# Short state-space calculations in the first modulation, and the turns of the state tiles cut in four and set between the steps of layer 1's linear attention

## What is computed

```python
lam = lax.complex(a_re, a_im)
dt = jnp.exp(log_step)[:, None]
a_bar = jnp.exp(lam * dt)
b_bar = ((a_bar - 1.0) / lam)[..., None] * lax.complex(b_re, b_im)
...
_, states = lax.associative_scan(s5_combine, (a_elems, bu), axis=1)
```

## Time and profile before

| | us |
|---|---|
| median of 3 runs | 1559.35 |
| lowest, highest | 1557.97, 1561.33 |
| the profiled execution | 1564.3 |
| its span (first to last instruction) | 1562.5 |
| PE busy in the span | 1386.5 |
| PEld busy | 1160.0 |
| DVE busy | 853.4 |
| POOL busy | 733.4 |
| ACT busy | 637.7 |

### The profile page before, as it was taken

One profiled execution on the slowest core, in us unless ns is written; L12 is line 12 of the kernel. 1 busy time (PEld: TensorE's weight loads), 2 busy tenths in 40 slices (PEclk: granted clock), 3 DMA queues, 4 the chain that ended last, 5 costly groups with the idle time before them and its releaser, 6 DMA issues.

```text
span 1562.5 us, 24541 instructions
## 1 busy us (share of the span) xinstructions
PE 1386.5 (89%) x10288; PEld 1160.0 (74%) x10288; DVE 853.4 (55%) x1213; ACT 637.7 (41%) x1002; POOL 733.4 (47%) x512
## 2 busy tenths in 40 slices
PE   5798999999999999688779899978799888799997
PEld 1654688777676887464768789968688777799996
DVE  1567415332333430756677666569899635488811
ACT  2445322433332333445325554656422123555542
POOL 0520044332222643140595767747645204499984
PEclk9899999999999999899899999989899999999998
DMA  8320133343443432130334334525222133355552
GB/s 335 120 68 14 42 95 94 108 175 122 161 161 120 137 95 81 40 95 28 108 94 135 108 122 132 162 84 178 79 83 82 56 95 109 94 185 181 188 176 82
DMA packets 49119, 180.79 MB, mean 116 GB/s; under 512 B 5489, under 2 KB 6513, under 8 KB 48625
## 3 DMA queue, kind: packets, MB, share of 16 engines
q1 hardware_dynamic: 48864, 177.13, 34.9%
q10 hardware_dynamic: 144, 2.10, 0.3%
HBM read 178.16 MB, written 1.05 MB: 115 GB/s over the span
## 4 chain that ended last, share of the span: by engine, by line
PE 67%; DVE 18%; ACT 5%; DMA 4%; POOL 3%; issue 2%; SPq 0%; ACTq 0%; DVEq 0%
PE ps L368 17%; PE ps L370 16%; PE ps L369 16%; PE ps L372 15%; DMA panels<-weights 3%; POOL panels_r L412 2%; DVE work L1830 2%; POOL panels_r L413 2%; ACT panels_hi L402 1%; PE ps L889 1%; DMA const_sb<-constants 1%; DVE small L937 1%; DVE work L732 1%; DVE work L1260 1%; DVE work L761 0%
## 5 line engine op out<-in xcount | busy, mean ns | idle before, releaser
L412 POOL TENSOR_TENSOR panels_r<-panels,panels_hi 128x512 fp32r<-128x512 f32 x254 | 376.0, 1480 | 808.5 <-ACT panels_hi L402 806.7
L369 PE MATMUL ps<-h_sb_r,panels_hi 128*128 128x256 f32 (+1 forms) x1408 | 453.3, 322 | 0.0
L402 ACT ACTIVATE panels_hi<-panels 128x1024 fp32r<-128x1024 f32 x254 | 267.5, 1058 | 416.8 <-PE ps L370 233.4
L413 POOL TENSOR_TENSOR panels_r<-panels,panels_hi 128x512 fp32r<-128x512 f32 x254 | 370.6, 1459 | 0.0
L368 PE MATMUL ps<-hi_sb_r,panels_hi 128*128 128x512 f32 (+1 forms) x784 | 279.8, 357 | 40.7 <-POOL panels_r L413 24.1
L369 PEld LDWEIGHTS ps<-h_sb_r,panels_hi 128*128 128x128 f32 x1408 | 276.9, 197 | 17.8 <-issue 0.7
L370 PE MATMUL ps<-hi_sb_r,panels_r 128*128 128x512 f32 (+1 forms) x784 | 273.2, 348 | 0.0
L368 PEld LDWEIGHTS ps<-hi_sb_r,panels_hi 128*128 128x128 f32 x784 | 153.9, 196 | 66.7 <-issue 19.2
L368 PE MATMUL ps<-h_sb_r,panels_hi 128*128 128x256 f32 x624 | 183.6, 294 | 12.1 <-DVE h_sb_r L594 7.6
L368 PE MATMUL ps<-work_r,panels_hi 128*128 128x256 f32 (+1 forms) x560 | 182.9, 327 | 10.2 <-POOL panels_r L413 6.0
L370 PE MATMUL ps<-h_sb_r,panels_r 128*128 128x256 f32 x624 | 179.5, 288 | 0.0
(11 more groups left out here) (323 smaller groups left out, 1820.4 us busy)
## 6 DMA issues: line engine op xcount, KB each, us to landing
panels<-weights SPq DMA_DIRECT2D x328, 512.0 KB, 3.6
x_sb<-x_in SPq DMA_DIRECT2D x1, 2048.0 KB, 8.1
x_sb<-x_in ACTq DMA_DIRECT2D x1, 2048.0 KB, 8.7
const_sb<-constants SPq DMA_DIRECT2D x1, 1216.0 KB, 10.6
out<-x_sb SPq DMA_DIRECT2D x2, 512.0 KB, 3.1
vec_sb<-vectors SPq DMA_DIRECT2D x1, 725.0 KB, 11.9
small<-c_in SPq DMA_DIRECT2D x1, 8.0 KB, 1.6
```

The costliest lines, as they stand in the source:

```text
L369: pe.matmul(o, lhsT.hi, rhs.lo, start=False, stop=False)
L402: act.activation(panels_hi[:, m:m + PANEL * P], panels[:, n:n + PANEL * P], ACT.Copy).then_inc(panel_rounded, 1)
L412: pool.tensor_tensor(panels_r[:, at:at + half], panels[:, at:at + half], panels_hi[:, m:m + half], ALU.subtract)
L413: pool.tensor_tensor(panels_r[:, at + half:at + 2 * half], panels[:, at + half:at + 2 * half], panels_hi[:, m + half:m + 2 * half], ALU.su ...
```

## The change

The short calculations (`s5_steps`, `s5_angles`, `s5_polar`, `s5_factors`) go from the head of layer 1 to the first modulation: the exponential ahead of the first `mod_copy` and the angles ahead of the first `mod_use`; the polar part behind that `mod_copy` and the factors behind that `mod_use`. They keep their results in other columns of `small`. The seven turns of 128x4096 become 28 units of 128x1024, seven per quarter of the state tiles, each waiting for the one before (u = 7q + n, with n as before). They leave the head; eight groups of them stand between VectorE's steps in the merge of layer 1. `whole_turns`, the buffer between, has the size of a quarter and lies in the context's half of `x_sb`. Each of the first four `s5_tables` waits for its own quarter.

```diff
@@ (these functions move here, ahead of first_modulation)
+        kept, brief = Room(small, 420), Room(small, 320)
+        mag, f_hi, f_lo, c_re, c_im = [kept(S5T) for _ in range(5)]
+        dt, th, turn, s_r, c_r = [brief(S5T) for _ in range(5)]
...
+        half_col = region(small, 36, 1)
+
+        def s5_steps(act):
+            act.wait_ge(vectors_loaded, 16)
+            act.activation(dt, vec("log_step"), ACT.Exp).then_inc(steps_done, 1)
+
+        def s5_angles(dve):
+            step = steps["dve"]
+            dve.memset(half_col, half_pi)
+            dve.wait_ge(vectors_loaded, 16)
+            dve.wait_ge(steps_done, 1)
...
@@ first_modulation
             def scalar(act):
+                s5_steps(act)
                 for i in range(len(MOD_FIRST)):
                     mod_copy(act, i, 6)
+                    if i == 0:
+                        s5_polar(act)
 
             def vector(dve):
+                s5_angles(dve)
                 for i, n in enumerate(MOD_FIRST):
                     mod_use(dve, i, 0, n, 7)
+                    if i == 0:
+                        s5_factors(dve)
@@ trunk
-            by_act, by_dve, head_products, head_scalar, head_vector = projection(f"inputs{l}", tiles, first=clear_pads, then=windows,
-                                        aside={("scalar", 0): s5_steps, ("vector", 0): s5_angles, ("scalar", 1): s5_polar,
-                                               ("vector", 1): s5_factors, ("vector", 3): s5_turns(0, 3), ("vector", 9): s5_turns(3, 4),
-                                               ("vector", 10): s5_turns(4, 5), ("vector", 11): s5_turns(5, 6)} if last else {})
+            by_act, by_dve, head_products, head_scalar, head_vector = projection(f"inputs{l}", tiles, first=clear_pads, then=windows)
@@ gla_and_merge
             def vector(dve):
                 steps["dve"](dve.memset(attn, 0.0))
                 inputs.head.vector(dve)
                 decay_minima(dve)
-                if inputs.turns is not None:
-                    inputs.turns(6, 7)(dve)
                 split_y(dve, 0)
...
                 mixes(dve, MIXES[l][0], MIXES[l][1])
+                turn(dve, 0, 6)
                 decayed(dve, 0)
                 mixes(dve, MIXES[l][1], cut[0])
                 scores_taken(dve, 0)
+                turn(dve, 6, 8)
                 mixes(dve, cut[0], cut[1])
                 states_summed(dve, 0)
+                turn(dve, 8, 11)
                 mixes(dve, cut[1], cut[2])
...
                 scores_taken(dve, 1)
+                turn(dve, 11, 13)
                 mixes(dve, cut[3], cut[4])
                 states_summed(dve, 1)
+                turn(dve, 13, 17)
                 mixes(dve, cut[4], cut[5])
                 outputs_added(dve)
+                turn(dve, 17, 20)
                 mixes(dve, cut[5], cut[6])
                 norm_inverse(dve)
+                turn(dve, 20, 22)
                 mixes(dve, cut[6], cut[7])
...
                 mixes(dve, MIXES[l][3], 3 * KD)
+                turn(dve, 22, 28)
@@ s5_turns, s5_tables
-        turns, whole_turns = cos_t, region(work, 10240, S5T, T)
+        turns, whole_turns = cos_t, of_context[:, 2:6, :]
...
-                t = each(const("step"), S5T)
-                for n in range(first, end):
-                    if n:
-                        dve.wait_ge(turned5, n)
+                t = each(const("step"), 4)
+                for u in range(first, end):
+                    n, q = u % 7, u // 7
+                    g = slice(4 * q, 4 * q + 4)
+                    part, of_step = turns[:, g, :], (f_hi, f_lo)[n // 3 % 2][:, g]
+                    if u:
+                        dve.wait_ge(turned5, u)
...
-                    if i == 0:
-                        act.wait_ge(turned5, 7)
+                    act.wait_ge(turned5, 7 * (i + 1))
```

More of the change, by code:

```diff
@@ new lines, in build @@
+        half_pi = 3.1415925 / 2
+        full = 6.283185
+        steps_done, arg_ready = sem("s5_steps_done"), sem("arg_ready")
+        half_col = region(small, 36, 1)
[7 more added lines that the diff above has]
+            dve.wait_ge(steps_done, 1)
+            step(dve.tensor_tensor(mag, vec("a_re"), dt, ALU.mult))
+            step(dve.tensor_tensor(th, vec("a_im"), dt, ALU.mult))
+            step(dve.tensor_scalar(turn, th, 1.0 / two_pi, None, ALU.mult))
+            step(dve.tensor_scalar(turn, turn, whole, None, ALU.add))
+            step(dve.tensor_scalar(turn, turn, -whole, None, ALU.add))
+            for c in (pi_a, pi_b, pi_c):
+                step(dve.scalar_tensor_tensor(th, turn, -c, th, ALU.mult, ALU.add))
+            step(dve.tensor_scalar(th, th, -3.1415925, 3.1415925, ALU.max, ALU.min))
+            step(dve.tensor_scalar(turn, th, 1.0 / two_pi, None, ALU.mult))
+            step(dve.tensor_scalar(f_hi, turn, 1.5 * 2 ** 11, None, ALU.add))
+            step(dve.tensor_scalar(f_hi, f_hi, -1.5 * 2 ** 11, None, ALU.add))
+            dve.tensor_tensor(f_lo, turn, f_hi, ALU.subtract).then_inc(arg_ready, 1)
@@ L1516, in scalar, with turn @@
                 gates(act, GATES[l][2], 3 * KD)
+            def turn(dve, first, end):
+                if inputs.turns is not None:
+                    inputs.turns(first, end)(dve)
             def vector(dve):
@@ L1570, in build @@
         sin_t, cos_t = s5_room(S5T, T), s5_room(S5T, T)
-        turns, whole_turns = cos_t, region(work, 10240, S5T, T)
         of_context = x_sb[:, :].rearrange("p (k s t) -> p k s t", s=2, t=T)[:, :, 1, :]
-        one = Room(small, 420)
-        dt, mag, th, turn, f_hi, f_lo, c_re, c_im, s_r, c_r = [one(S5T) for _ in range(10)]
-        two_pi = 2.0 * float(np.pi)
-        pi_a = 6.28125
-        pi_b = float(np.float32(round((two_pi - pi_a) * 2 ** 20) / 2 ** 20))
-        pi_c = float(np.float32(two_pi - pi_a - pi_b))
@@ L1649, in vector @@
                     elif n in (1, 5):
[L1650 removed]
+                        ins = dve.tensor_scalar(whole_turns, part, whole, None, ALU.add)
                     else:
[L1652 removed]
+                        ins = dve.scalar_tensor_tensor(part, whole_turns, whole, part, ALU.subtract, ALU.subtract)
                     ins.then_inc(turned5, 1)
```

86 lines of the change are left out of this document (33 added, 53 removed).

## The result

The changed kernel takes **1549.16 us** (median of 9 runs, 1542.57 to 1554.63) against 1560.75 (9 runs, 1556.36 to 1561.88) for the kernel before on the same chip: ratio 0.9932, 95% interval 0.9911 to 0.9953. Gains in us are worked out from this ratio here, of 1560 us: 10.6 less. Run once more, later and beside other kernels, it gave 1550.36 us (6 runs) and 0.9934 (0.9911 to 0.9958), 10.3 us less. The forecast was 11.4 us less.

What follows compares the result with a forecast made beforehand. The prediction blamed TensorE's gaps in layer 1's head on late POOL, delayed by ScalarE's wait and whole turns. Head gain 22.1 less merge cost 10.7 gave 11.4 us: 1559.35 - 11.4 = 1548.0 us, its own range 1542 to 1555.

Steps and rivals of the forecast that it cites:

- The head gives 22.1: Layer 1's head: three TensorE gaps of 8.59, 1.90 and 7.71 us and the half-clock restarts go, 22.1 us less.
- the stand: Layer 1's head: ScalarE waits 9.91 us for small angle operations; removing this ends TensorE's first gap, 8.59 us plus 2.5 clock.
- Units 0 to 5, 6.0: Merge, ahead of the first decayed: taking turns with POOL delays VectorE, so TensorE waits some 6.0 us for the scores.
- Clock behind it, 1.4: Merge: TensorE restarts at a lower clock after its wait for the first scores, costing 1.4 us.
- Units 11 and 12, 2.3: Merge, ahead of mix 11 and the summed states: with two POOL pieces they exceed their 1.99 us cover, costing 2.3 us.
- Units 20 and 21, 1.0: Merge, ahead of a mix and the norm's product: half of a 2.2 us excess over cover counted, 1.0 us.
- Merge, 10.7: Layer 1's merge: the moved units cost 6.0 + 1.4 + 2.3 + 1.0 = 10.7 us.
- Last group, 0: Units 22 to 27, behind the merge's last mix: VectorE is idle 28.12 us there, so they cost 0.
- POOL becomes the merge's bound: Rival, merge: units before the last group hold POOL off, adding 22.8 us; 1571 us, slower, chance 0.06.
- The gaps hold: Rival, merge: POOL's backlog misses units 0 to 5, later groups are covered, merge costs 2.9; 1540 us, chance 0.22.
- the second and third gap stay: Rival, layer 1's head: something other than turns keeps POOL late, only 8.59 + 2.5 comes back; 1559 us, chance 0.05.
- POOL is met everywhere: Rival, merge: 75% of units 6 to 21 each meet a POOL piece, merge costs 19 us; 1556 us, chance 0.12.

Runs made afterwards that it cites:

- fitted: The changed kernel with other numbers of units in the same eight places, two left empty and twelve units behind the last mix; ratio 0.9919 to the kernel before.
- without_turns: The changed kernel with 24 of its 28 units left out, the four that stay in the last group; ratio 0.9843 to the kernel before.
- cut_in_head: The kernel before with each whole turn cut into four quarter operations at its old place in layer 1's head; ratio 1.0001.
- small_only: The kernel before with only the short calculations moved to the start, whole turns staying uncut in layer 1's head; 1541.38 us, ratio 0.9873.

## Why the prediction came out right, step by step

- **Small operations, 0**: right. 0.63 us of idle time is left ahead of the first `mod_use` and 7.39 ahead of the second, and the modulation ended no later than before.
- **The head gives 22.1**: 22.4 measured, in both executions. All three gaps and the half-clock restarts went, and POOL's pieces are 1.29 us but for a few beside other operations of VectorE. But the parts don't stand for what each cause is worth. The prediction gave the stand 8.59 us and 2.5 of clock, and the turns 9.61 and 1.4. Taken away alone, the stand's removal gives 15.2 us and the turns' removal 12.0, 27.2 for a whole of 22.4: both feed on the same lead of POOL. The prediction didn't ask what each edit is worth alone, and so didn't see that the first alone is the better kernel.
- **Units 0 to 5, 6.0**: too high. TensorE's wait is 4.61 us (4.79 in the second execution), and 0.83 of that stood there before, so some 3.8. The mechanism, taking turns with POOL up to the backlog's end and again in the new panels, is as told.
- **Clock behind it, 1.4**: mis-sized, and not only behind the stand. The first four matmuls behind the wait take 1.12 us instead of 0.60, so the half clock is there. But leaving the six out gave back 3.5 to 5.1 us in all, of which TensorE's idle time is 3.9 to 4.2, so that 1.2 us of clock or none came back, while 2.9 us of longer busy time stand in the merge even without units.
- **Units 11 and 12, 2.3**: the second states' wait is 2.94 us where it was 1.54, so 1.4. The prediction named a wait of 3 to 4 us as its sign here; it is just under that.
- **Units 20 and 21, 1.0**: too low. The norm's product waits 2.92 us where it waited 0.45, so 2.5, and the whole of the 2.2 would have been near it. Halving the term because items lie between was wrong; TensorE had worked them off by then.
- **Merge, 10.7**: 13.1 in the first execution, 11.6 in the second, of which 9.0 to 10.5 are the units. The waits were put at 9.3 us and are 7.7; the clock was put at 1.4 and is 3.7 to 5.5, the difference in TensorE's busy time. That is the term that was mis-sized most, and why the clock is lower stays open.
- **Last group, 0**: right for six units (the output stretch is 0.4 us longer), and not for twelve, as fitted shows.
- **The sum**: -22.4 + 11.6 to 13.1 + 0.4 is -10.4 to -8.9, measured -10.6 and -10.3. The forecast of 1548.0 is 1.2 us from the median, closer than the terms were: waits put too high and clock put too low cancel, and so far it is luck that the sum fits.
- **The rivals.** *POOL becomes the merge's bound* falls: TensorE's waits for POOL in the merge are the 3.0 us of before. The rule of the Trainium skill ("SBUF — State Buffer", section "Summary: rules for kernel authors") that stood beside this rival holds in the trace as to blocking, 2.20 us for a unit beside POOL and 1.23 alone, but what was late by it was VectorE, not POOL. *The gaps hold*, with 2.9 us for the merge, and *the second and third gap stay* fall with the rows above. *POOL is met everywhere* would have cost 19 us in the merge, more than the 11.6 to 13.1 measured.

## What to carry to other kernels

Place work that fills an engine by what is queued behind it and who waits for that, item by item; the idle total of a stage says little, since the same 28 units cost 9 to 10.5 us in the merge in one order and nothing that can be told from without_turns in another. Where two engines block each other by whole instructions, cutting an instruction can move the wait from one to the other, as in cut_in_head; look first whether the engine that was cut has idle time there. And try each half of a change alone: two edits that free the same lead don't add up, and one of them may only cost, as the turns' move did here. Last, split a stage's time into idle and busy: what the waits don't explain may be clock.

## What the runs showed of the hardware

A tiny VectorE operation pays the whole turn of POOL too. In cut_in_head (and the kernel before) one of the factor operations takes 0.18 us before POOL starts its panel pieces at 760.95, and another of the same size 1.22 beside the pieces, while those stay at 1.3:

```profile
760.59 0.18 DVE L1623 TENSOR_TENSOR small<-vec_sb 128x16 f32<-128x16 f32 x1
...
769.74 1.22 DVE L1633 TENSOR_TENSOR small<-small 128x16 f32<-128x16 f32 x1
```

At the program's start all fifteen take 0.17 to 0.25 us each. So such a chain of short operations is better put where POOL is quiet.

The granted clock in a stage depends on more than what happens within it: 0.94 and 0.99 for the merge of without_turns and of small_only. And the length of a gap alone doesn't tell its cost in clock: the clock is full behind 3.57 us in small_only and half behind 8.59 us, but behind the same wait of 2.63 us it is 1.00 in small_only, 0.84 in the kernel before and 0.67 in without_turns.
